# Two transformer-like blocks on one core: the second half with tokens on the partitions

## What is computed

```
x1  = layer_norm(alpha*x + mix(x), ln1)                # first block: convolution, gated linear attention
ffn = sum over the 2 of 64 experts chosen by a token: w * (silu(x1@w1[e]) * (x1@w3[e])) @ w2[e]
x2  = layer_norm(alpha*x1 + ffn, ln2_g, ln2_b)         # alpha = 2 ** 0.25
u   = rms_norm(x2, norm_mix_pre);  z = u @ w_in_2      # second block
merged = sum over 4 branches of sigmoid(u @ w_gate_2[b]) * (y_b @ w_branch_2[b])
h   = x2 + rms_norm(merged @ w_out_2, norm_mix_post)
u   = rms_norm(h, norm_ffn_pre)
out = h + rms_norm((silu(u @ Wg) * (u @ Wu)) @ w_ffn_down_2, norm_ffn_post)
```

## Time and profile before

| | |
|---|---|
| median of 3 runs | 1896.68 us (1893.74 to 1898.21) |
| profiled execution, own time | 1897.18 us |
| its span | 1895.4 us |
| PE busy | 1558.4 us, 82% of the span |
| PEld | 1073.6 us, 57% |
| DVE | 615.2 us, 32% |
| ACT | 400.4 us, 21% |
| POOL | 4.7 us |
| chain that ended last | PE 62%, DMA 21%, DVE 10%, issue 3%, ACT 2% |

### The profile page before, as it was taken

The page is one execution under the profiler, slowest core; times in us unless marked ns, Lnnn a source line. Parts: engine busy times, 40 slices in busy tenths (PEclk is TensorE's granted clock), DMA queues, the critical chain, the costliest instruction groups (busy, mean ns, idle before and its releaser), DMA issues.

```text
span 1895.4 us, 22082 instructions
## 1 busy us (share of the span) xinstructions
PE 1558.4 (82%) x9046; PEld 1073.6 (57%) x9046; DVE 615.2 (32%) x1084; ACT 400.4 (21%) x600; POOL 4.7 (0%) x5
## 2 busy tenths in 40 slices
PE   7998969677777777767677677777999999979996
PEld 7788858533332233322333323332888878869996
DVE  3687942501111011110111101112353667254753
ACT  3555120500100001000010000100421432245542
POOL 0000000000000000000000000000000000000000
PEclk9999989778788897888888788888999999989998
DMA  9432337269999999999999999998332314335530
GB/s 311 173 134 89 134 127 277 89 252 429 428 427 430 427 430 425 428 430 428 429 428 428 429 427 430 427 430 340 112 128 89 134 45 178 133 122 189 179 112 23
DMA packets 90693, 525.06 MB, mean 277 GB/s; under 512 B 6514, under 2 KB 14834, under 8 KB 66052
## 3 DMA queue, kind: packets, MB, share of 16 engines
q1 hardware_dynamic: 90320, 523.39, 68.2%
q10 hardware_dynamic: 308, 0.78, 0.1%
HBM read 523.10 MB, written 1.05 MB: 277 GB/s over the span
## 4 chain that ended last, share of the span: by engine, by line
PE 62%; DMA 21%; DVE 10%; issue 3%; ACT 2%; SPq 1%; DVEq 0%; ACTq 0%
PE psum L323 15%; DMA shared<-in_w 11%; DMA ring<-in_w 10%; PE psum L1065 8%; PE psum L1046 6%; PE psum L1032 6%; PE psum L381 5%; PE psum L383 5%; PE psum L382 5%; PE psum L1076 3%; DVE arena L749 3%; PE psum L605 1%; PE psum L344 1%; SPq L1317 1%; DVE shared L1818 1%
## 5 line engine op out<-in xcount | busy, mean ns | idle before, releaser
L1046 PE MATMUL psum<-ring,arena 128*32 128x512 f32 x1024 | 281.4, 683 | 46.8 <-DMA ring<-in_w 46.8
L1046 PE MATMUL psum<-shared,arena 128*32 128x512 f32 x1024 | 273.5, 683 | 39.8 <-DMA shared<-in_w 26.9
L381 PE MATMUL psum<-parts 128*128 128x256 f32 (+1 forms) x832 | 246.7, 297 | 11.8 <-DVE parts L459 7.1
L382 PE MATMUL psum<-parts 128*128 128x256 f32 (+1 forms) x832 | 243.5, 293 | 0.0
L383 PE MATMUL psum<-parts 128*128 128x256 f32 (+1 forms) x832 | 243.5, 293 | 0.0
L1065 PE MATMUL psum<-ring,shared 128*32 128x512 f32 x512 | 175.8, 765 | 61.8 <-DMA ring<-in_w 61.8
L323 PE MATMUL psum<-arena,ring 128*128 128x256 f32 x960 | 215.0, 386 | 11.6 <-DMA ring<-in_w_in 11.3
L323 PEld LDWEIGHTS psum<-arena,ring 128*128 128x128 f32 x960 | 185.1, 194 | 38.4 <-issue 12.8
L1065 PE MATMUL psum<-shared 128*32 128x512 f32 x512 | 160.8, 749 | 40.3 <-DMA shared<-in_w 28.7
L381 PEld LDWEIGHTS psum<-parts 128*128 128x128 f32 x832 | 162.0, 195 | 21.2 <-issue 13.7
L1046 PEld LDWEIGHTS psum<-shared,arena 128*32 128x32 f32 x1024 | 70.6, 123 | 176.6 <-issue 143.3
(11 more groups left out here) (207 smaller groups left out, 1514.3 us busy)
## 6 DMA issues: line engine op xcount, KB each, us to landing
shared<-in_w SPq DMA_DIRECT2D x96, 2048.0 KB, 16.4
ring<-in_w SPq DMA_DIRECT2D x96, 2048.0 KB, 23.7
ring<-in_w_in SPq DMA_DIRECT2D x18, 2048.0 KB, 8.8
ring<-in_w_ffn_gate_up SPq DMA_DIRECT2D x11, 2048.0 KB, 8.1
ring<-in_w_gate SPq DMA_DIRECT2D x8, 2048.0 KB, 8.9
ring<-in_w_ffn_down SPq DMA_DIRECT2D x5, 2048.0 KB, 7.8
ring<-in_w_out SPq DMA_DIRECT2D x4, 2048.0 KB, 8.0
ring<-in_w_gla_out SPq DMA_DIRECT2D x2, 2048.0 KB, 8.6
```

Of the source, the lines that this page charges most:

```text
L381: pe.matmul(out, w[0], x[0], start=start, stop=False)
L382: pe.matmul(out, w[0], x[1], start=False, stop=False)
L1046: m = pe.matmul(ps[slots, bank, :], V.picked[:, k, slots], w[e][:, k, :], start=(k == 0), stop=(k == DT - 1))
```

## The change

From the MoE's sum on, the residual stream (`total`, x2, `h`, the output) lies as 2 tiles of [128 tokens x 1024 channels]. The statistics of the five norms are then 128x1: by `bn_stats` and `bn_aggr` for ln2, by ACT's Square with an accumulated output for the others. All six means on PE are gone. The gains, now along the free axis, are read as 128x1024 broadcasts (512 KB each, five loads on SP's queue: the two of ln2 behind the MoE's first 8 slabs, two ahead of the out projection's weights once `start_exp` is signalled, the last at the sixth up slab). `total` starts as alpha*x1, written by POOL (one TENSOR_SCALAR of 128x2048) from the token rows that the kernel has anyway for picking; DVE's memset of `total` is gone. Where u is needed with channels on the partitions (ahead of z0 and of the feed-forward), PE transposes it in 16 pieces of 128x128 (`turn_u`). The out projection and the down projection hold the activations still and stream 512 columns of weights. The memory's mk and mv come right after the MoE. The last 4 units' work for the second tile of tokens is done after the first tile is complete. The output is stored in four transfers of 256 KB (2 KB rows), one for each tile and half. On DVE (not in the cut diff) the transposes ahead of z0 are read from PSUM as 4 operations of 128x512 that also multiply by the gain.

```
         for j, bank in enumerate(MOE_BANK["put"]):
-            for part in range(2):
-                k = 2 * j + part
-                m = pe.matmul(ps[:, bank, part * T:(part + 1) * T], V.y[:, k * P:(k + 1) * P], V.wsel_t,
-                              start=True, stop=True)
+            t, half_d = divmod(j, 2)
+            m = pe.matmul(ps[:, bank, :], V.wsel_t[:, t * P:(t + 1) * P], V.y[:, half_d * 512:half_d * 512 + 512],
+                          start=True, stop=True)
...
-    h2 = K.tiles(1, DT)
-    act_squares(K, L, K.tiles(3, DT), h2, "ln2_centred", "ln2_squares")
-    act_std(K, L, B, "ln2_var", K.A(4, T), "ln_eps")
-    act_affine(K, L, K.tiles(0, DT), h2, "ln2_g", "ln2_b", "ln2_scaled", "x2")
+    x2, scratch, u_rows = K.tiles(0, TT, D), K.tiles(4, TT, D), K.tiles(3, TT, D)
+    act.preload_act_table(ACT.Sqrt)
+    for t in range(TT):
+        act.wait_ge(S("ln2_stats"), t + 1)
+        L.done(act.activation(K.stat("sd", t), K.stat("mean_var", 2 * t + 1), ACT.Sqrt, bias=K.c("ln_eps")), S("row_sd"))
+    for t in range(TT):
+        act.wait_ge(S("x2"), t + 1)
+        L.done(act.activation(scratch[:, t, :], x2[:, t, :], ACT.Square, accum_out=K.stat("squares", t)), S("row_squares"))
+        L.done(act.activation(K.stat("sd", t), K.stat("squares", t), ACT.Sqrt, bias=K.c("rms_eps"), scale=1.0 / D),
+               S("row_sd"))
+        act.wait_ge(S("pre_rstd"), t + 1)
+        L.done(act.activation(u_rows[:, t, :], x2[:, t, :], ACT.Copy, scale=K.stat("rstd", t)), S("u_rows"))
...
-    x1, total, h2 = K.tiles(0, DT), K.tiles(2, DT), K.tiles(1, DT)
-    dve.wait_ge(S("x1"), DT)
-    for m in range(DT):
-        L.done(dve.scalar_tensor_tensor(h2[:, m, :], x1[:, m, :], ALPHA1, total[:, m, :], ALU.mult, ALU.add),
-               S("pre_ln2"))
-    dve_centre(K, L, B, "ln2_mean", h2, "ln2_centred")
-    dve_rstd(K, L, B, "ln2_var", K.A(4, T))
-    for m in range(DT):
-        L.done(dve.tensor_tensor(h2[:, m, :], h2[:, m, :], K.A(4, T), ALU.mult), S("ln2_scaled"))
+    dve.sem_inc(S("puts_read"), 1)
+    total, x2 = V.total, K.tiles(0, TT, D)
+    for t in range(TT):
+        for half in range(2):
+            L.done(dve.bn_stats(K.stat("bn", 12 * t + 6 * half, 6), total[:, t, 512 * half:512 * half + 512]), step)
+        L.done(dve.bn_aggr(K.stat("mean_var", 2 * t, 2), K.stat("bn", 12 * t, 12)), S("ln2_stats"))
+    K.wait_gain(dve, "ln2_b")
+    for t in range(TT):
+        L.done(dve.scalar_tensor_tensor(x2[:, t, :], total[:, t, :], K.stat("mean_var", 2 * t), K.gain("ln2_g"),
+                                        ALU.subtract, ALU.mult), step)
+        dve.wait_ge(S("row_sd"), ROW_SD["ln2"] + t + 1)
+        L.done(dve.reciprocal(K.stat("rstd", t), K.stat("sd", t)), step)
+        L.done(dve.scalar_tensor_tensor(x2[:, t, :], x2[:, t, :], K.stat("rstd", t), K.gain("ln2_b"),
+                                        ALU.mult, ALU.add), S("x2"))
...
+    for t in range(TT):
+        for half in range(2):
+            B.wait_read(pool, f"turn_x{t}_{half}")
+    pool.tensor_scalar(K.A(2), K.A(1), ALPHA1, None, ALU.mult).then_inc(S("total_added"), 1)
...
+    for t in range(TT):
+        K.banks1.wait_full(sp, f"logits{t}")
+    for name in ("ln2_g", "ln2_b"):
+        K.load_gain(sp, name)
...
+    pe.wait_ge(S("puts_read"), 1)
...
+    def turn_u(name, rows, t):
+        for half in range(2):
+            b = B.take(pe, f"{name}{t}_{half}")
+            for j in range(4):
+                m = pe.transpose(ps[:, b, j * P:(j + 1) * P], rows[:, t, (4 * half + j) * P:(4 * half + j + 1) * P],
+                                 K.c("ident"))
+            m.then_inc(B.full[b], 1)
     mem_values(0)
-    pe_mean_by_tile(K, pe, B, "pre_ms", K.tiles(3, DT), "pre_squares")
     mem_values(1)
     R.last_group["mem"] = "mv1"
+    for t in range(TT):
+        pe.wait_ge(S("u_rows"), t + 1)
+        turn_u("turn_u", K.tiles(3, TT, D), t)
     w = K.slab(R.wait_landed(pe, "z0"))
     for m in range(4):
         b = B.take(pe, f"hq{m}")
         for k in range(DT):
-            if m == 0:
-                pe.wait_ge(S("u"), k + 1)
+            if m == 0 and k % 4 == 0:
+                pe.wait_ge(S("u"), 3 + k // 4)
...
-    pe.wait_ge(S("merged"), 4 * DT)
     for s in range(2):
-        pe_slab_tiles(K, pe, B, R, f"o{s}", names("oz", 4 * s, 4), V.merged)
-
-    pe_mean_by_tile(K, pe, B, "post_ms", K.tiles(3, DT), "post_squares")
-    pe_mean_by_tile(K, pe, B, "ffn_ms", K.tiles(3, DT), "ffn_squares")
+        w = K.slab(R.wait_landed(pe, f"o{s}"))
+        for t in range(TT):
+            b = B.take(pe, f"oz{t}_{s}")
+            for k in range(DT):
+                if s == t == 0:
+                    pe.wait_ge(S("merged"), 3 * DT + k + 1)
+                m = pe.matmul(ps[:, b, :], V.merged[:, k, t * P:(t + 1) * P], w[:, k, :], start=(k == 0),
+                              stop=(k == DT - 1))
+            m.then_inc(B.full[b], 1)
+        R.last_group[f"o{s}"] = f"oz1_{s}"
+    for t in range(TT):
+        pe.wait_ge(S("u2"), t + 1)
+        turn_u("turn_u2", K.tiles(1, TT, D), t)
     sp = Split(K)
     for n in range(UNITS_UP):
         b = B.take(pe, f"ff{n}")
         pe.wait_ge(S("unit_low"), n + 1)
         w = sp.shaped(n, 0), sp.shaped(n, 1)
         for k in range(DT):
-            if n == 0:
-                pe.wait_ge(S("u_low"), k + 1)
+            if n == 0 and k % 4 == 0:
+                pe.wait_ge(S("u_low"), 3 + k // 4)
             m = three_passes(pe, ps[:, b, 0:T], [p[:, k, :] for p in w], [p[:, k, :] for p in sp.u], k == 0, k == DT - 1)
         m.then_inc(B.full[b], 1)
-    down = []
+    down = {(t, half): B.take(pe, f"dn{t}_{half}") for t in range(TT) for half in range(2)}
+    def down_tile(f, t):
+        n = UNITS_UP + f
+        for half in range(2):
+            cols = slice(512 * half, 512 * half + 512)
+            ins = three_passes(pe, ps[:, down[t, half], :], [p[:, f, t * P:(t + 1) * P] for p in sp.hidden],
+                               [sp.part(n, i)[:, cols] for i in range(2)], f == 0, f == FT - 1)
+            if f == FT - 1:
+                ins.then_inc(B.full[down[t, half]], 1)
+        return ins
     for f in range(FT):
-        n = UNITS_UP + f
-        pe.wait_ge(S("unit_low"), n + 1)
+        pe.wait_ge(S("unit_low"), UNITS_UP + f + 1)
         pe.wait_ge(S("hidden_low"), f + 1)
-        for m in range(DT):
-            if f == 0:
-                down.append(B.take(pe, f"dn{m}"))
-            ins = three_passes(pe, ps[:, down[m], 0:T], [sp.part(n, i)[:, m * P:(m + 1) * P] for i in range(2)],
-                               [p[:, f, :] for p in sp.hidden], f == 0, f == FT - 1)
-            if f == FT - 1:
-                ins.then_inc(B.full[down[m]], 1)
-            elif m == DT - 1:
-                ins.then_inc(S("down_read"), 1)
-    pe_mean_by_tile(K, pe, B, "last_ms", K.tiles(3, DT), "last_squares")
+        ins = down_tile(f, 0)
+        if f < FT - PART_BUFS:
+            down_tile(f, 1).then_inc(S("down_read"), 1)
+    for f in range(FT - PART_BUFS, FT):
+        down_tile(f, 1)
...
-    for m in range(DT):
-        evac(f"oz{m}", K.tiles(2, DT)[:, m, :])
-        squares(K.tiles(3, DT)[:, m, :], K.tiles(2, DT)[:, m, :], "post_squares")
-    act_std(K, L, B, "post_ms", V.rstd, "rms_eps")
-    act_squares(K, L, K.tiles(3, DT), V.h, "h2", "ffn_squares")
-    act_std(K, L, B, "ffn_ms", V.rstd, "rms_eps")
-    for m in range(DT):
-        act.wait_ge(S("u2"), m + 1)
-        L.done(act.activation(sp.u[0][:, m, :], V.u[:, m, :], ACT.Copy), S("u_high"))
...
+    z = K.tiles(2, TT, D)
+    K.wait_gain(dve, "n_ffn_pre")
+    for s in range(2):
+        for t in range(TT):
+            b = B.wait_full(dve, f"oz{t}_{s}")
+            cols = slice(512 * s, 512 * s + 512)
+            dve.wait_ge(S("row_squares"), 2 + 2 * s + t + 1)
+            tt(z[:, t, cols], ps[:, b, :], K.gain("n_mix_post")[:, cols], ALU.mult)
+            if s == 0:
+                ts(K.stat("part", t), K.stat("squares", 2 * t), 1.0 / D, RMS_EPS, ALU.mult, ALU.add, S("row_part"))
+            else:
+                dve.wait_ge(S("row_sd"), ROW_SD["post"] + t + 1)
+                L.done(dve.reciprocal(K.stat("rstd", t), K.stat("sd", t)), step)
+                for half in range(2):
+                    dve.sem_inc(B.free_of(f"oz{t}_{half}"), 1)
+                stt(V.h[:, t, :], z[:, t, :], K.stat("rstd", t), V.h[:, t, :], ALU.mult, ALU.add, S("h2"))
+    for t in range(TT):
+        dve.wait_ge(S("row_sd"), ROW_SD["ffn"] + t + 1)
+        L.done(dve.reciprocal(K.stat("rstd", t), K.stat("sd", t)), step)
+        stt(K.tiles(1, TT, D)[:, t, :], V.h[:, t, :], K.stat("rstd", t), K.gain("n_ffn_pre"), ALU.mult, ALU.mult, S("u2"))
+    for t in range(TT):
+        for half in range(2):
+            g = f"turn_u2{t}_{half}"
+            b = B.wait_full(dve, g)
+            dve.wait_ge(S("u_high"), 2 * t + half + 1)
+            part = [p[:, 4 * half:4 * half + 4, t * P:(t + 1) * P] for p in sp.u]
```

(21 more changed lines are left out.)

142 lines of the change are left out of this document (82 added, 60 removed).

## The result

The changed kernel took 1851.21 us, median of 4 runs (1849.03 to 1851.6), the kernel before beside it 1895.21 (1891.92 to 1898.21): a ratio of 0.9758, interval 0.9733 to 0.9784. 1853.3 was forecast, 43.4 us less than before; 44.0 is what it gained against the median beside it. The profiled pair differs by 45.6 (spans 1895.4 and 1849.8).

A forecast was written before the change was run, and what follows sets the result against it. Transfers bound the MoE and PE most later stretches, neither the stages between. Terms +2.6 - 10.5 - 19.5 - 4.2 - 11.8 = -43.4 us, from the median of 1896.68, gave 1853.3 us, range 1846 to 1862.

The forecast's parts named there:

- Start of the MoE: Ahead of the MoE, DVE waits for POOL's new operation for total, delaying routing, first picks and later transfers: +2.6 us.
- the lock: Ahead of the MoE, a two-input DVE operation waits for the end of POOL's operation; bounds nothing to 4.1 us.
- The sign that it named: Ahead of the MoE, POOL's operation takes 3 us in the new trace and DVE's at 366.6 ends with it.
- The 2.2 us by the Trainium skill: Alternative estimate of POOL's operation ahead of the MoE, one-input operations at about line rate; the term would be +1.9.
- The loop: In the MoE, four puts of 512 columns for eight of 256 stream the same columns: 0 us.
- the slower rival: In the MoE, puts make DVE or PE wait in all 16 quads; from 2.7 us a quad the sum turns; chance 0.02.
- MoE to z0: Between MoE and z0, memory groups no longer wait behind the means; PE and norms legs meet within 0.5 us: -10.5 us.
- the rival's 0.3: In several norms, ACT's accumulated outputs cost 0.3 us each, seven on the path, +2.1 us, giving 1855.4; chance 0.07.
- The middle stretch: From z0 to the out projection, PE's own stretch shifts as a whole with the earlier z0: 0 us.
- Out projection and norms: Out projection starts merge by merge (-2.8) and both norms behind it shorten (-16.7): -19.5 us together.
- Down projection: In the down projection, 264 matmuls of 512 columns replace 528 of 256: -4.2 us; a skill formula gives 0.7 gain.
- End: After the last matmul, only tile 1's last half and a smaller last transfer count, 6.6 us against 18.4: -11.8 us.

The follow-up runs named there:

- total_late: Changed kernel with POOL's operation for total moved behind its memory operation, after the first picks are copied: 1847.06 us, ratio 0.9742.
- pool_twice: Changed kernel with POOL's operation for total done twice, one after the other: profiled span 1853.9 us.
- again_after2: The changed kernel run a second time without edits: 1850.82 us, ratio 0.9774.
- warm: Changed kernel with 11 unread 256-column matmuls on PE between out projection and transposes ahead of the up projection: 1850.83 us, ratio 0.9776.
- warm_more: As warm, plus one unread matmul ahead of the second tile's transposes and four behind them: 1852.35 us, ratio 0.9792.
- order_undone: Changed kernel with both token tiles of the down projection kept together to the last unit: 1853.32 us, ratio 0.9792.
- all_in: late_filled with the order of turn_early: 1844.38 us, ratio 0.9747.
- late_filled: both_late with the fills of warm_more and 5 unread matmuls in PE's wait for the pooled rows: 1844.27 us, ratio 0.9742.
- both_late: Changed kernel with both of POOL's operations, total and the memory scaling, behind the first picks: 1847.06 us, ratio 0.9736.
- down_256: Changed kernel with the down projection's 512-column matmuls split into two of 256 for 20 of 22 units: 1856.44 us, ratio 0.9798.
- again_before: The kernel before, profiled a second time without edits: 1897.86 us.
- turn_early: Changed kernel with tile 0's reciprocal for u earlier on DVE and its transposes between two memory groups on PE: 1856.3 us, ratio 0.9802.

## Why the prediction was right, and where by luck

The measured median is 2.1 us under the forecast: 1.5 because the kernel before had 1895.21 beside it and not 1896.68, 0.6 by the gain.

**Start of the MoE (+2.6, measured +2.68): the lock is right and shown** by total_late and pool_twice, **its size came by chance.** Two of three streams gave POOL 3.0 us, and the record is 5.39, longer than that of the operation with two inputs, 4.50, which the prediction had taken as the upper bound. The sign that it named, 3 us on POOL and DVE going on at its end, did not come: DVE was held until 3.8 us after POOL's start, 1.6 before its end (3.8 in all eight profiles in which `total`'s operation comes first). Which DVE operation was caught differs too, and block 1 ahead of it varies: with the same code to this place the first w1 matmul started between 391.28 and 392.99 in seven profiles. The 2.2 us by the Trainium skill (GPSIMD Engine Reference, "Engine selection") are further off.

**The loop (0, measured +0.74): right.** From the first w1 matmul to the end the MoE took 926.6 to 928.7 in all 14 profiles, those with the old put stage among them, so 0.74 is spread, and no quad loses the 2.7 us of the slower rival.

**MoE to z0 (-10.5, measured -9.8).** bn_stats took 0.71 where a reduction's 0.69 stood in, 128x1024 operations 1.28 instead of 1.22, and ACT's accumulated output came as a record of its own, 0.19, less than the rival's 0.3. None of this set the stage: PE's leg binds. The term that was too small is the one behind the memory groups, forecast 2.9 and measured 3.4 (1335.1 to 1338.51), since z0 waited 1.37 for three of DVE's reads behind the transposes.

**The middle stretch (0, measured -3.6): the missing term.** Its length over all profiles, with the clock's falls in it:

| profile | middle stretch | low clock near |
|---|---|---|
| after, again_after2, total_late, warm, warm_more, order_undone, all_in | 279.7 to 279.9 | neither |
| late_filled | 281.3 | 8-column matmuls |
| before | 283.4 | 8-column matmuls |
| pool_twice | 282.7 | behind the wait for the pooled rows |
| both_late, down_256, again_before | 285.9 to 286.1 | both |
| turn_early | 287.6 | both |

But for the 5 unread matmuls of two kernels, the matmuls in it are the same in all. down_256, whose code in this stretch is that of the changed kernel, took 285.9 where the changed kernel took 279.7 twice. So the 3.6 us belong to the executions compared and not to the work changed: without them the profiled pair differs by 41.9, or by 42.7 if the MoE's 0.74 is left out as spread, so the sum of -43.4 was 0.7 to 1.5 too large. The lowest of all 36 runs of the kernel before took 1891.75 and the lowest of the nine of the changed one 1849.03, 42.7 apart, which agrees. The median's 44.0 cannot tell: that it met 43.4 so closely is luck. Whether the change makes the falls rarer isn't shown (both profiles of the kernel before have falls, neither of the changed kernel). What decides in which executions the clock falls stays open: kernels that differ only in their ends (down_256) had falls that the changed kernel has in neither of its two profiles, and one of the nine runs of the changed kernel was 7 us over the rest.

**Out projection and norms (-19.5, measured -19.2).** The first part took 27.7 us as forecast, without the 1.9 at low clock of the earlier trace rows. The loss of 1.8 at the up projection's start was 1.6: 1655.42 to an effective 1656.99. It came close by another way than the one forecast: 3.3 to 5.1 us at the low level were taken, and from PE's restart at 1650.77 it lasted 8.0, of which the transposes had the first part. (In the earlier trace rows the matmuls at 1307.41 are already the fast ones, 0.60 against 1.07, so that stretch was 5.0 us and not longer than 5.1.) warm_more gives the whole price of that low clock, 1.9.

**Down projection (-4.2, measured -4.1).** By rows of the same form; the formula's 0.7 is refuted for this stream by down_256. The page that it is from, TensorE: Matmul & The Clock Gate of the Trainium skill, gives it under "Back-to-back issue gap" for an isolated matmul, which the prediction left out.

**End (-11.8, measured -12.3).** The last transfer took 0.4 us less than the forecast 2.9. Of the whole, the order of the units gave 2.0, which the prediction had not priced by itself.

## What to carry to other kernels

Statistics along the free axis turn chains of 128x256 roots, reciprocals and PE means into 128x1 operations; where PE waits for such a chain, cost it by hand-overs between engines and by the order of tiles in each queue. Price a matmul by a row of its own form and width. When several waits of 2 to 5 us are left on PE, read the clock of the stretches behind them in more than one profile before a difference of a few us between two kernels is explained, and try unread matmuls in all waits ahead of such a stretch together: ahead of the up projection, filling only the longest brought 0.3 us, filling all 1.9.
